# Expert down weights in 2 MB transfers with four rows to a partition

## What is computed

```python
def expert_block(args):                 # one block of tokens of one expert
    xblk, e = args
    hg = xblk @ w_gu[e] + b_gu[e]       # w_gu[e] is 1024 x 2048: 8 MB
    x_glu, x_lin = hg[:, :D_FF], hg[:, D_FF:]
    x_glu = jnp.minimum(x_glu, SWIGLU_LIMIT)
    x_lin = jnp.clip(x_lin, -SWIGLU_LIMIT, SWIGLU_LIMIT)
    act = x_glu * jax.nn.sigmoid(SWIGLU_ALPHA * x_glu) * (x_lin + 1.0)
    return act @ w_down[e] + b_down[e]  # w_down[e] is 1024 x 1024: 4 MB
...
y = yb.reshape(P, D) * gate_pad[:, None]
out = jnp.zeros((T + 1, D), y.dtype).at[tok_pad].add(y)[:T]
```

## Time and profile before

| | us |
|---|---|
| median of 3 runs | 2307.92 |
| lowest, highest | 2306.47, 2313.52 |
| profiled execution, its own time | 2306.57 |
| span within it | 2304.7 |

### The profile page before, as it was taken

One profiled execution on the slowest core, in us unless ns is written; L12 is line 12 of the kernel. 1 busy time (PEld: TensorE's weight loads), 2 busy tenths in 40 slices (PEclk: granted clock), 3 DMA queues, 4 the chain that ended last, 5 costly groups with the idle time before them and its releaser, 6 DMA issues.

```text
span 2304.7 us, 34153 instructions
## 1 busy us (share of the span) xinstructions
PE 2212.9 (96%) x11074; PEld 1269.1 (55%) x11075; DVE 794.1 (34%) x1727; ACT 371.7 (16%) x849; POOL 358.4 (16%) x2324
## 2 busy tenths in 40 slices
PE   6999999999999999999999899999999899999987
PEld 3464458888544688998888533333333233333323
DVE  1133655555561435873124422121112112111212
ACT  3222222111001322220234210000001000000001
POOL 0000010000001000000000033333333333333332
PEclk9999999999999999999999899999999999999999
DMA  9721342222574706548851499899899989989996
GB/s 380 253 74 55 101 138 91 92 92 75 181 256 163 237 5 210 171 156 301 272 184 56 158 408 422 353 422 422 361 418 422 421 357 422 422 358 422 422 422 285
DMA packets 196206, 602.76 MB, mean 262 GB/s; under 512 B 11042, under 2 KB 128034, under 8 KB 146850
## 3 DMA queue, kind: packets, MB, share of 16 engines
q1 hardware_dynamic: 193728, 599.04, 67.9%
q10 hardware_dynamic: 2402, 2.67, 0.4%
HBM read 600.62 MB, written 1.05 MB: 261 GB/s over the span
## 4 chain that ended last, share of the span: by engine, by line
PE 81%; DMA 11%; SPq 3%; DVE 2%; ACT 1%; issue 1%; POOL 0%; POOLq 0%; ACTq 0%; DVEq 0%
PE bank L371 52%; PE bank L972 27%; DMA wring<-in_w_gu 10%; SPq L2306 3%; DMA wring<-in_ev_w_in 1%; ACT big L1154 1%; DVE wring L1575 1%; PE bank L1004 1%; ACT tmp L1154 0%; DVE hT L1575 0%; PE bank L997 0%; PE bank L679 0%; POOL xT L2296 0%; PE bank L473 0%; PE bank L945 0%
## 5 line engine op out<-in xcount | busy, mean ns | idle before, releaser
L972 PE MATMUL bank<-wring,big 128*64 128x512 f32 x3456 | 773.1, 596 | 41.1 <-DMA wring<-in_w_gu 32.7
L972 PEld LDWEIGHTS bank<-wring,big 128*64 128x64 f32 x3456 | 235.2, 137 | 529.7 <-issue 411.2
L371 PE MATMUL bank<-hT,wring 128*128 128x256 f32 (+2 forms) x1888 | 450.3, 392 | 4.6 <-POOL hT L2269 2.2
L371 PEld LDWEIGHTS bank<-hT,wring 128*128 128x128 f32 x1888 | 319.5, 191 | 118.1 <-issue 85.9
L371 PE MATMUL bank<-big,wring 128*128 128x256 f32 (+1 forms) x1096 | 341.8, 473 | 0.0
L2292 POOL COPY big<-hT 128x8 f32 x2240 | 310.2, 200 | 109.1 <-issue 109.0
L371 PEld LDWEIGHTS bank<-big,wring 128*128 128x128 f32 x1096 | 207.5, 190 | 130.3 <-issue 114.0
L371 PE MATMUL bank<-wring 128*128 128x256 f32 (+1 forms) x1408 | 246.2, 328 | 3.1 <-DVE wring L1575 3.0
L371 PEld LDWEIGHTS bank<-wring 128*128 128x128 f32 x1408 | 215.8, 191 | 23.1 <-DVE wring L1575 4.5
L1154 ACT ACTIVATE big<-bank 128x256 f32<-128x256 f32 (+3 forms) x239 | 89.5, 390 | 765.9 <-PE bank L997 385.4
L1578 DVE TENSOR_SCALAR big<-bank 128x512 f32<-128x512 f32 (+1 forms) x74 | 50.2, 678 | 447.8 <-PE bank L972 446.6
(11 more groups left out here) (170 smaller groups left out, 1242.1 us busy)
## 6 DMA issues: line engine op xcount, KB each, us to landing
wring<-in_w_gu SPq DMA_DIRECT2D x256, 1024.0 KB, 18.7
wring<-in_w_down SPq DMA_DIRECT2D x128, 1024.0 KB, 18.6
wring<-in_ffn_w_up SPq DMA_DIRECT2D x44, 1024.0 KB, 5.1
wring<-in_mod_w SPq DMA_DIRECT2D x24, 1024.0 KB, 14.8
wring<-in_mod_w SPq DMA_DIRECT2D x48, 512.0 KB, 4.5
wring<-in_ffn_w_down SPq DMA_DIRECT2D x16, 1024.0 KB, 5.2
wring<-in_w_ada SPq DMA_DIRECT2D x16, 1024.0 KB, 5.3
wring<-in_w_in SPq DMA_DIRECT2D x14, 1024.0 KB, 11.9
```

Of the source, the lines that this page charges most:

```text
L371: ins = pe.matmul(o, l, r, start=start, stop=stop, skip_group_check=True)
L972: ins = pe.matmul(o, l, r, start=start, stop=stop, skip_group_check=True)
```

## The change

The four transfers of 1 MB for the down weights become two of 2 MB. Each fills two neighbouring ring slots: rows 4p to 4p+3 of a stretch of 512 rows of `w_down` go to partition p, so a partition gets one piece of 16 KB in place of two of 8 KB. On TensorE `wpair` waits once for a pair, ahead of slots 8 and 10, where `wslot` waited for each; the products and their number stay the same. `turn_act` reads `AV` with a step of 4. On SyncE a pair is issued when its second slot is free. The gate and up weights are as before.

```diff
+            def wpair(s, e):
+                i, uses, last = places[base + s]
+                pe.wait_ge(w_full[i], e * 16 + 16 * (uses + 1))
+                return wring[:, i:i + 2, :].rearrange("p a (j n) -> p (a j) n", j=2)
...
-                    at = 256 * (c // 2) + c % 2
-                    ins = pe.transpose(bank[6 + c // 2][:, P * c:P * c + P], AV[:, at:at + 255:2], ident)
+                    ins = pe.transpose(bank[6 + c // 2][:, P * c:P * c + P], AV[:, c:c + 509:4], ident)
...
-                    ws = wslot(GUC + s, e).rearrange("p (j n) -> p j n", j=2)
+                    if s % 2 == 0:
+                        pair[0] = wpair(GUC + s, e)
...
-                            xmm(halves(bank[6], i), kchunk(AC, k), ws[:, j, T2 * i:T2 * i + T2], k == 0, k == 7,
+                            xmm(halves(bank[6], i), kchunk(AC, k), pair[0][:, k % 4, T2 * i:T2 * i + T2], k == 0, k == 7,
...
+            def down_pair(s, e):
+                rows_of = slice(256 * (s - GUC), 256 * (s - GUC) + 512)
+                if isinstance(e, int):
+                    src = w_down[0, e, rows_of, :].rearrange("(p j) n -> p (j n)", p=P)
+                else:
+                    src = w_down[0, bass.ds(e, 1), rows_of, :].rearrange("a (p j) n -> p (a j n)", p=P)
+                i = places[n0 + s][0]
+                assert places[n0 + s + 1][0] == i + 1
+                sp.dma_start(wring[:, i:i + 2, :].rearrange("p a n -> p (a n)"), src).then_inc(w_full[i], 16)
...
+            def following(done, e):
+                for s in range(GUC):
+                    sp.wait_ge(G("moe_used"), done * RING + (s + 1))
+                    load(n0 + s, up(s, e), SLOT)
+                for s in range(GUC, RING, 2):
+                    sp.wait_ge(G("moe_used"), done * RING + (s + 2))
+                    down_pair(s, e)
```

More of the change, by code:

```diff
@@ L974, in xmm @@
                     ins.then_inc(inc, 1)
+            pair = [None]
+            def wpair(s, e):
+                i, uses, last = places[base + s]
+                pe.wait_ge(w_full[i], e * 16 + 16 * (uses + 1))
+                return wring[:, i:i + 2, :].rearrange("p a (j n) -> p (a j) n", j=2)
             def halves(bk, i):
@@ L2347, in _, with up @@
                     load_mod(k)
-            def expert(s, e):
-                if s < GUC:
+            def up(s, e):
+                if isinstance(e, int):
                     return w_gu[0, e, P * s:P * s + P, :]
-                return w_down[0, e, 256 * (s - GUC):256 * (s - GUC) + 256, :].rearrange("(p j) n -> p j n", p=P)
+                return w_gu[0, bass.ds(e, 1), P * s:P * s + P, :].rearrange("a p n -> p (a n)")
+            def down_pair(s, e):
+                rows_of = slice(256 * (s - GUC), 256 * (s - GUC) + 512)
+                if isinstance(e, int):
+                    src = w_down[0, e, rows_of, :].rearrange("(p j) n -> p (j n)", p=P)
[4 more added lines that the diff above has]
+                sp.dma_start(wring[:, i:i + 2, :].rearrange("p a n -> p (a n)"), src).then_inc(w_full[i], 16)
             for s in range(RING):
                 wait_free(n0 + s)
-                load(n0 + s, expert(s, 0), SLOT)
+                if s < GUC:
+                    load(n0 + s, up(s, 0), SLOT)
+                elif s % 2:
+                    down_pair(s - 1, 0)
+            def following(done, e):
[5 more added lines that the diff above has]
+                    down_pair(s, e)
             sp.wait_ge(G("tables"), 1)
@@ L2360, in _ @@
                 e = sp.value_load(turn_of[0:1, bass.ds(turn, 1)], min_val=0, max_val=NE - 1)
[L2361 to L2367, removed]
+                following(done, e)
             for c in range(DC):
```

## The result

The changed kernel took 2312.18 us (median of 14 runs, 2307.64 to 2317.5), the kernel before 2308.07 us beside it (14 runs, 2302.66 to 2313.52). The ratio is 1.0016 with a 95% interval of 1.0009 to 1.0024: by it 3.7 us slower, between 2.1 and 5.5. I had said 0.5 us faster, 2307 in a range of 2302 to 2313, with 0.83 for "within 0.3%". The time lies in the range and within 0.3%, but the sign is wrong: the interval excludes both no change and my sum.

What follows compares the result with a forecast made beforehand. The prediction took the transfers to set the end of the experts. Packets -4.3, first refill +1.2, later refills +1.6, TensorE's waits +1.0 and transposes 0 summed to -0.5 us: 2307 us, range 2302 to 2313.

Steps and rivals of the forecast that it cites:

- The bound: Over the experts: transfers set the end; TensorE's work counts only between last arrival and next free slot, and at the end.
- the two signs: Rounds at the transfers' pace (29.8 us) moving over 0.3 us, or TensorE's 25.5 us changing by more than 4.3 us.
- The packets' gain: Down-weight transfers in steady flow: 16 KB packets save 0.07 us per pair, 62 pairs, -4.3 us.
- The first refill: First round, queue run dry: the pair must wait for slot 9 and begins 1.2 us later; bounds 0.6 and 1.8.
- The refills after the standstills: Four restarts of the transfers: the first pair's lead shrinks to 1.95 us, costing 0.4 us each, +1.6; bounds 0 and 4.8.
- TensorE waits for a pair: Ahead of slot 10, before four standstills and in the last block: the pair lands 0.2 us late, +1.0 us in all.
- The transposes with step 4: TensorE's weight loads from `AV`: at most 0.27 us more in a block, taken as 0 in the sum.
- Fewer issues: SyncE's queue: two fewer issues per expert, at 0.33 us each, are worth nothing.
- refills are much worse: Rival: each pair into a nearly dry queue costs 1.2 us, the first refill 1.8; +3.8 more, about 2311; chance 0.07.

Runs made afterwards that it cites:

- late_issue: Kernel before, all transfers still 1 MB, but slot 8 issued only when slot 9 is free and slot 10 when slot 11 is: 2312.99 us, ratio 1.0019.
- first_pair_only: Changed kernel's layout, slots 8 and 9 as one 2 MB transfer, slots 10 and 11 as single 1 MB transfers: 2312.49 us, 1.0019 against the kernel before.
- second_pair_only: Changed kernel's layout, slots 8 and 9 as single 1 MB transfers, slots 10 and 11 as one of 2 MB: 2308.73 us, 0.9999 against the kernel before.
- layout4_single: Kernel before with four rows to a partition and transposes of step 4, but 1 MB transfers each at its own time: 2308.25 us, ratio 0.9997.
- pair_8k: Changed kernel's two 2 MB transfers, but with two 8 KB pieces per partition and transposes of step 2: 2317.6 us, 1.0035 against the kernel before.
- late_more: Kernel before with 1 MB transfers, slots 8 and 9 issued only when slot 10 is free, 10 and 11 when slot 11 is: 2315.67 us, ratio 1.0032.

## Why the prediction was wrong

My sum was -4.3 + 1.2 + 1.6 + 1.0 + 0 = -0.5 us.

- **The bound: right.** The transfers set the experts' time and TensorE's pace did not move: 25.51 us as before, the experts in full flow 0.16 us shorter. Neither of the two signs by which I would have called the prediction wrong appeared; the direction was wrong all the same.
- **The packets' gain, -4.3: near, by luck in part.** Full flow went from 29.82 to 29.67 us, 0.08 for a pair where I had 0.07, and the bytes moved at 424 GB/s as said. All 62 pairs together gained 5.0 us, more than my upper bound of 4.3. The packets fell by 196,206 - 186,990 = 9216 where I wrote 7936: there are 64 pairs with the first expert's, and 1024 small packets went as well. But I counted 62 pairs. In the five experts that end a stretch, the path starts at the arrival of slot 7, and the two pairs land behind it: their gain makes nothing earlier. From the arrival of slot 7 to the next issue it took 15.14 us before and 15.36 after: the wait of 0.22 us and no gain. That is 5 x 0.16 = 0.8 us which the sum had and the kernel has not; 5.0 - 0.8 = 4.2 is near my 4.3 because the two misses cancel. I had written myself that TensorE works from its last arrival on, and then counted all pairs alike.
- **The first refill, +1.2: agrees, but not shown.** +1.15 in the table, with 0.16 gained in it, so 1.3 lost. The pair landed at 1342.69 + 7.6 = 1350.3, predicted "near 1350". But the three values before spread over 2.0 us, and `late_issue`, which issues slot 8 as late, took only 0.1 us more than their mean.
- **The refills after the standstills, 4 x 0.4 = +1.6: the term that failed.** Measured 4 x 1.04 = +4.2, within its bounds of 0 and 4.8; the 2.6 us between the two alone turn the sum from a gain into a loss. I had the right mechanism and the right place (a lead that shrinks from 3.7 to 1.95 us), and a price taken from one 2 us stretch at 295 GB/s, which gave 0.6, then cut to 0.4 without a row behind the cut. The price of a dip has to be read from the landings of two neighbours, and the stretch showed part of it: `late_issue` pays 1.6 us for the same lateness with 1 MB transfers. `late_issue`, `first_pair_only` and `second_pair_only` show that lateness at slot 8 costs time without any pair, and that a pair at slots 10 and 11 alone leaves slot 8 as it was. That the size of the first pair adds nothing is not shown.
- **TensorE waits for a pair, 5 x 0.2 = +1.0: right.** 10.74 against 10.52 us, 5 x 0.22 = 1.1; with the 0.16 of above it makes the 0.36 us between last landing and next issue and the 0.4 at the end. No wait ahead of slot 8. (I had written that the standstills last 8 us; from packet to packet they took 6.65 us before and 7.0 after.)
- **The transposes with step 4, 0: right.** 212 ns against 209, and `layout4_single` at 0.9997. The Trainium skill, "SBUF — State Buffer", section "Door 1: The DMA port swizzle", would have made four fp32 the step at which a price begins; here it begins at two and does not grow, so on TensorE's weight loads the measurement decides against it.
- **Fewer issues, 0: right.** `pair_8k` issues as few and saves nothing in full flow.

With the measured terms the sum is -5.0 + 1.3 + 4.2 + 1.9 = +2.4, against +2.0 in the traces and +3.7 (2.1 to 5.5) in the times. The 0.4 us between the first two stand in the second expert's row of the table, -0.65 where 0.16 was gained. The rival "refills are much worse" held 1.2 us for each and the end at 2311; I gave it 0.07. Its price was nearer than mine.

## What to carry to other kernels

Merging two transfers delays the first half's issue to the second half's free slot. In a full queue this costs the transfers nothing and larger rows bring their 0.5% per expert, though the consumer may wait for the merged transfer where it had the first half before (0.22 us, five times). Where the queue has just restarted, the lead is what matters, so count the restarts before counting the transfers. Where a loss varies between 0 and 2 us from one restart to the next, read it from several traces, and hold their sum against the median of many executions. And when a bound is "the last arrival, then TensorE", a gain behind that arrival is worth nothing there: count it only where the path passes through it.

## What the runs showed of the hardware

- A transfer issued about 2 us ahead of its turn into a nearly dry queue loses 0.8 to 1.6 us on average, single ones from 0 to 2.3 us, though a transfer issued into an empty queue begins about 1 us after its issue (1667.35 to the first packet at 1668.34). Issued 2.7 us ahead it lost 0.14 us on average over four refills, 2.9 to 4.5 us ahead (slot 8 of the "before" traces) nothing in 12. There is no sharp bound: with the second pair alone, that pair lost nothing in four refills with leads of 2.3 to 2.8 us, while in the changed kernel three second pairs with 2.8 to 2.9 us lost 0.6 to 1.05. Why 2 us aren't enough, no run here shows.
- The loss does not grow with more delay: 1.6 us (`late_issue`) and 1.5 us (`late_more`).
- In the traces a first pair of 2 MB loses less (0.76 us with 16 KB packets, 1.3 with 8 KB) than a single late slot of 1 MB (1.6 us); the times point the other way (6.8 us against 4.4 in all). With this scatter no run separates the size.
- In full flow one engine takes 0.611 us for each 16 KB packet (4.89 us for the eight of a pair), where two of 8 KB take 0.621. The 4.8 us from issue to landing of a lone 1 MB transfer do not show in full flow at all; fewer transfers of the same packets (`pair_8k`) gained nothing.
